# Two splits, three clears and a PSUM bank at the head of the first mixer's projections

## The chip, the cores and the metric

The kernel runs on one core of one Trainium2 chip. The metric is the device time of one execution in microseconds (us); lower is better. Times are compared as medians of several executions, and where the stage is looked at from inside, in one profiled execution.

## The reference, cut to what matters

Two transformer blocks run one after the other on 512 tokens of width 1024, in fp32. The change touches only the head of the first block's mixer:

```python
mod = (silu(c) @ w_ada + b_ada)                    # shift1, scale1, gate1, ...
h = rms_norm(x, norm1_w) * (1.0 + scale1) + shift1
p = h @ w_in                                       # 1024 x 3592
qkv = silu(causal_depthwise_conv(p[..., 0:1536], conv_qkv_w))   # four taps
z = p[..., 1536:2048]
a, b = p[..., 2048:2052], p[..., 2052:2056]        # four heads each
g = -exp(a_log) * softplus(a + dt_bias)            # the "row inputs"
beta = sigmoid(b)
# g is summed up inside chunks of 64 tokens, then the gated delta rule runs
```

Everything behind it (gated delta rule, short convolution, output projection, three feed-forward layers, the second block's attention and RWKV mixer) is not touched.

## The kernel before, in words

Activations lie transposed: channels on the partitions, tokens along the free dimension. Every fp32 product is made of three fp32r products. Operand and weight are each split in a high part and a low rest: `HH` and `HL` for the normed input, `WH` and `WL` for the weight.

**Slabs.** Weights come in slabs of 128 x 1024 (one 128-column tile of output, eight k-tiles), in the fixed order `ORDER`, through a ring of four raw buffers `RAW` (the profile's RAWS). Those that are split are numbered in `CUT`: 0 is `ab` (the columns of a and b, 64 wide, half a slab), then `w_in` in the order `IN_ORDER = [4, 5, 6, 7, 0, 1, 2, 3, 8, ...]` as numbers 1, 2, 3 and on. In the text, split number c is called cut c. For each cut ScalarE copies the slab to `WH[c % 3]` (L1767), for which it waits for the matmuls of cut c-3; GpSimd then makes `WL[c % 3]` by four subtractions of 128 x 256 (L2274; two for `ab`) and counts up `w_lo`; TensorE waits for `w_lo` and issues 24 matmuls of 128 x 512, three for each k-tile (L533). SyncE loads the next slab into a raw buffer when that buffer's split is done.

**The head.** The mixer's modulation columns are made first (L568 are its last matmuls, into banks 0 and 1). VectorE reads them (`ada_mod`) and then goes through the norm: for each k-tile a product to `TMP` (L1166), ScalarE's rounding of it to `HH` (L1829), VectorE's rest to `HL` (L1159, counted by `n_lo`). Cut 0 and cut 1 are interleaved on TensorE, k-tile by k-tile: 24 matmuls each, 48 in all. Each k-tile waits for its `n_lo`.

**Banks.** The results of `ab` and of the `w_in` slabs alternate between PSUM banks 0 and 1 by their place in the list `MAIN`: `ab` is place 0 (bank 0), cut 1 place 1 (bank 1), cut 2 place 2 (bank 0). From place 3 on a product waits until the one two places ahead has been read (`cv_tap` for a convolved slab). Place 2 waits for the two readers of `ab`: `row_d.at("tx")` on VectorE (L1239) and `row_a.at("beta")`, a sigmoid on ScalarE (L1883).

**ScalarE in the loop.** For i = 1, 2, ... it makes `WH` of cut i+2 (`begin`), at i = 1 does its part of the row inputs (sigmoid to `ROW`, absolute value, exponential and logarithm in `RT`, `NEA`; two table loads), then `evict(i - 1)`: it copies a finished bank to `STG` (L1852) and its last tap to `TMP` (L1854). From i = 2 on it then applies silu (L1860) and a square (L1863). The `RT` temporaries lie in `TMP[0]` and `TMP[1]`, so the tap of slabs 0 to 2 waits for `row_d.at("rg")`, VectorE's scan of the row inputs (L1251), the last reader of `RT`. VectorE does the row inputs' own steps (L1239, L1242, L1246, L1251) ahead of its first convolution (L1225, three instructions a slab).

**GpSimd at the head.** It adds up the squares, waits for the last modulation column (`ada_col.at(1)`), clears `STG` edges, `ROW` and `ST` (L2299 to L2301), and then starts to split slabs.

Of the kernel before, what the change touches and what calls it, by code (L numbers as in the profile page):

```python
# [59 lines left out]
IN_ORDER = [4, 5, 6, 7, 0, 1, 2, 3] + list(range(8, 28))  # L60
# [20 lines left out]
CUT = {}  # L81
# [46 lines left out]
def finish(stream):  # L128
    for _ in stream:
        pass  # L130
# [12 lines left out]
def program(nc, xT, metaT, cols, consts, slabs, lup, gup, out):  # L143
    f32, f32r = mybir.dt.float32, mybir.dt.float32r
    ALU, ACT = mybir.AluOpType, mybir.ActivationFunctionType
    ve, ae, ge, te, se = nc.vector, nc.scalar, nc.gpsimd, nc.tensor, nc.sync
# [5 lines left out]
    def steps(name, *names):  # L152
        return Steps(sem(name), *names)

    def count(name):
        return Count(sem(name))

    def sbuf(name, shape, dt=f32, st=top):
        return st.enter_context(nc.sbuf_tensor(name, shape, dt))


    PS = top.enter_context(nc.psum_tensor("PS", [128, 8, 512], f32))
# [4 lines left out]
    def bank(i):  # L167
        return PS[:, i, :]
# [16 lines left out]
    TMP = [sbuf(f"TMP{i}", [128, T2]) for i in range(3)]  # L185
# [18 lines left out]
    Z = sbuf("Z", [128, 4, 512], st=m1)  # L204
    YS = sbuf("YS", [128, 4, 512], st=m1)
    ROW = sbuf("ROW", [64, 512], st=m1)
    NEA = sbuf("NEA", [4, 1], st=m1)
    STG = [sbuf(f"STG{i}", [128, 3 + 512], st=m1) for i in range(2)]
    RT = [TMP[i][0:64, 0:512] for i in range(2)]
    COLT = sbuf("COLT", [128, 4, 64], st=m1)  # L210
    EGC = sbuf("EGC", [128, 4, 4], st=m1)
    BEG = sbuf("BEG", [128, 4, 4], st=m1)
# [97 lines left out]
    ada_acc, ada_col, ada_mod = count("ada_acc"), count("ada_col"), count("ada_mod")  # L310
# [13 lines left out]
    n_h, n_hi, n_lo, n_out = count("n_h"), count("n_hi"), count("n_lo"), count("n_out")  # L324
# [9 lines left out]
    cv_ev, cv_tap, cv_si = count("cv_ev"), count("cv_tap"), count("cv_si")  # L334
    cv = steps("cv", "t0", "t1", "t2")
    row_d = steps("row_d", "tx", "sp", "gg", "rg")
    row_a = steps("row_a", "beta", "abs", "exp", "ln", "nea")
# [43 lines left out]
    rg = [steps(f"rg{i}", "c1", "c2") for i in range(2)]  # L381
# [20 lines left out]
    def col(name, i=0, p0=0, p1=128):  # L402
        return CV[p0:p1, COLS[name] + i:COLS[name] + i + 1]
# [117 lines left out]
    def tensor():  # L521
# [67 lines left out]

        def main_bank(what, j):  # L590
            i = MAIN_AT[what, j]
            if i == 2:
                te.wait_ge(*row_d.at("tx"))
                te.wait_ge(*row_a.at("beta"))
            elif i > 2:
                te.wait_ge(*main_read(*MAIN[i - 2]))
            return bank(i % 2)
# [530 lines left out]
    def vector():  # L1128
# [107 lines left out]
        for i in range(1, 10):  # L1236
            if i == 1:
                ve.wait_ge(*gemm.at(CUT["ab", 0]))
                ve.tensor_scalar(RT[0][0:4, :], PS[0:4, 0, :], col("dtb", 0, 0, 4), None,  # L1239
                                 ALU.add).then_inc(*row_d.up("tx"))  # L1240
                ve.wait_ge(*row_a.at("ln"))
                ve.scalar_tensor_tensor(RT[0][0:4, :], RT[0][0:4, :], 0.0, RT[1][0:4, :], ALU.max,  # L1242
                                        ALU.add).then_inc(*row_d.up("sp"))
                ve.wait_ge(*row_d.at("sp"))
                ve.wait_ge(*row_a.at("nea"))
                ve.tensor_scalar(RT[0][0:4, :], RT[0][0:4, :], NEA[:, 0:1], -1.0, ALU.mult,  # L1246
                                 ALU.mult).then_inc(*row_d.up("gg"))
                ve.wait_ge(*row_d.at("gg"))
                ve.wait_ge(*zeros.at("row"))
                ve.wait_ge(s_k1, 32)  # L1250
                ve.tensor_tensor_scan(ROW[0:4, :], YS[0:4, 0, :], RT[0][0:4, :], 0.0, ALU.mult,  # L1251
                                      ALU.add).then_inc(*row_d.up("rg"))
                ve.wait_ge(*row_d.at("rg"))
            finish(convolve(i - 1))
            if i == 3:
                ve.wait_ge(*row_t.at(0))
                ve.tensor_copy(COLT[:, :, :], h4(PS[:, 2, 0:256])).then_inc(*row_c.up("colt"))
            elif i == 5:
                ve.wait_ge(*row_e.at(0))
                ve.tensor_tensor(BEG[:, :, :], EGC[:, :, :], COLT[:, :, 32:36], ALU.mult).then_inc(*row_c.up("beg"))  # L1260
            elif i == 8:
                finish(unit_heads(0))
# [493 lines left out]
    def scalar():  # L1756
# [13 lines left out]
        def begin(which, j, ahead=2, cap=len(CUTS)):  # L1770
            split_to(min(CUT[which, j] + ahead, cap))
# [72 lines left out]
        def evict(i):  # L1844
            j = IN_ORDER[i]
            b = bank(MAIN_AT["w", j] % 2)
            ae.wait_ge(*gemm.at(CUT["w_in", j]))
            if i >= 2:
                ae.wait_ge(*cv.at("t2", i - 2))
            else:  # L1850
                ae.wait_ge(*zeros.at(f"stg{i}"))
            ae.activation(STG[i % 2][:, 3:515], b, ACT.Copy).then_inc(*cv_ev.up(i))  # L1852
            ae.wait_ge(*(cv_si.at(i - 3) if i >= 3 else row_d.at("rg")))
            ae.activation(TMP[i % 3][:, 0:512], b, ACT.Identity, scale=col("convq", 36 + j)).then_inc(*cv_tap.up(i))  # L1854

        def silu(i):
# [20 lines left out]
        begin("w_in", IN_ORDER[0], 1)  # L1877
        for i in range(1, 10):
            begin("w_in", IN_ORDER[i], 1)
            if i == 1:  # L1880
                ae.wait_ge(*gemm.at(CUT["ab", 0]))
                ae.wait_ge(*zeros.at("row"))
                ae.activation(ROW[32:36, :], PS[32:36, 0, :], ACT.Sigmoid).then_inc(*row_a.up("beta"))  # L1883
                log_and_exp()
                ae.wait_ge(*row_d.at("tx"))
                ae.activation(RT[1][0:4, :], RT[0][0:4, :], ACT.Abs).then_inc(*row_a.up("abs"))
                ae.wait_ge(*row_a.at("abs"))
                ae.activation(RT[1][0:4, :], RT[1][0:4, :], ACT.Exp, scale=-1.0).then_inc(*row_a.up("exp"))
                ae.wait_ge(*row_a.at("exp"))
                ae.activation(RT[1][0:4, :], RT[1][0:4, :], ACT.Ln, bias=1.0).then_inc(*row_a.up("ln"))  # L1890
                ae.activation(NEA[:, :], col("alog", 0, 0, 4), ACT.Exp).then_inc(*row_a.up("nea"))
            evict(i - 1)
            if i == 7:
                begin("w_in", IN_ORDER[8], 1)
                finish(l2_roots(0))
            if i > 1:
                silu(i - 2)
            if i == 4:
                ae.wait_ge(*row_c.at("colt"))
                ae.activation(EGC[:, :, :], COLT[:, :, 0:4], ACT.Exp).then_inc(*row_e.up(0))  # L1900
# [10 lines left out]
        def evictions():  # L1911
            for i in (10, 11):
                yield i - 10
                evict(i)
            for u in range(4):
                yield 2 + u
                ae.wait_ge(*gemm.at(CUT["w_in", 12 + u]))
                ae.activation(Z[:, u, :], bank(MAIN_AT["w", 12 + u] % 2), ACT.Copy).then_inc(*z_ev.up(u))
            for u in range(4):
                yield 6 + u  # L1920
                ae.wait_ge(*gemm.at(CUT["w_in", 16 + 3 * u]))
                ae.wait_ge(*row_d.at("rg"))
                ae.activation(YS[:, u, :], bank(MAIN_AT["w", 16 + 3 * u] % 2), ACT.Copy).then_inc(*sc_ev.up(u))
            for u in range(4):
                yield 10 + u
                ae.wait_ge(*sc.at("y", u))
                ae.wait_ge(*gemm.at(CUT["w_in", 27]))
                ae.activation(HH[:, 4 + u, NM:T2], YS[:, u, :], ACT.Copy).then_inc(*cat1_hi.up(u))
# [334 lines left out]
    def gpsimd():  # L2263
        split = [0]

        def split_to(c):

            while split[0] <= min(c, len(CUTS) - 1):
                s, i = split[0], LOAD[CUTS[split[0]]]
                n = ORDER[i][2]  # L2270
                ge.wait_ge(*w_hi.at(s))
                for a in range(0, n, 256):
                    p = slice(a, a + 256)
                    ins = ge.tensor_tensor(WL[s % NS][:, p], RAW[i % NR][:, p], WH[s % NS][:, p].bitcast(f32),  # L2274
                                           ALU.subtract)
                ins.then_inc(*w_lo.up(s))
                split[0] += 1
# [8 lines left out]
        def add_squares(q, n, *tiles):  # L2286
            for k in tiles:
                ge.wait_ge(*squared(q, k))
                if k > 1:
                    ge.wait_ge(*added(q, k - 1))  # L2290
                ge.tensor_tensor(SQA[:, 0:n], SQA[:, 0:n], TMP[k % 3][:, 0:n],  # L2291
                                 ALU.add).then_inc(*n_acc.up(added(q, k)[1] - 1))


        ge.memset(EPSC[:, :], EPS).then_inc(*epsc.up(0))
        add_squares(0, T1, *range(1, 7))
        ge.wait_ge(*ada_col.at(1))
        for i in range(2):
            ge.memset(STG[i][:, 0:3], 0.0).then_inc(*zeros.up(f"stg{i}"))  # L2299
# [304 lines left out]
```

## Time and profile before

| what | value |
|---|---|
| median of 3 runs | 1966.74 us (1963.08 to 1975.59) |
| the profiled execution's own time | 1970.3 us |
| its span in the trace | 1969.1 us |
| TensorE busy in the span | 1892.1 us (96%) |
| mean granted TensorE clock | 0.984 |

The span is the trace's, from the first to the last instruction, and 1.2 us shorter than the execution's own time. The profiled execution stands 3.6 us above the median and inside the range of the runs. Engines in the rows are PE (TensorE), PEld (its weight loads), DVE (VectorE), ACT (ScalarE), POOL (GpSimd), SP (SyncE).

### The profile page before, as it was taken

The numbers are of one execution on the slowest core, as the hardware profiler recorded it, in microseconds if no ns is written. First come the engines' busy times: TensorE is split into PE (matmuls) and PEld (weight loads), VectorE is DVE, ScalarE is ACT, GpSimd is POOL, SyncE is SP. The second block draws the span as 40 slices with busy tenths as digits, with TensorE's granted clock in tenths as the row PEclk, the third lists the DMA queues.
The fourth block names the chain that finished last, engine by engine and source line by source line (L and its number), as shares of the span: only waits on it lengthen the run. The fifth ranks groups of instructions, "written<-read, shape, count | busy, mean of one in ns | idle before, by whom it ended". The sixth has DMA issues, their size and how long they took to land.

```text
span 1969.1 us, 32734 instructions
## 1 busy us (share of the span) xinstructions
PE 1892.1 (96%) x13848; PEld 1618.7 (82%) x13848; DVE 688.7 (35%) x1066; ACT 688.7 (35%) x1048; POOL 960.6 (49%) x1262
## 2 busy tenths in 40 slices
PE   5999999999999999999999999998999899999998
PEld 4777887677888888999999999997776678888886
DVE  6466564222111011232220025666776432222101
ACT  3653222332322234222222233426665442222222
POOL 3553222645545565655555555543332655555553
PEclk8999998999999999999999999999999999999999
DMA  7243421323332332332232242210001423332321
GB/s 298 75 144 134 140 77 34 107 78 143 123 97 89 93 96 80 103 92 92 86 92 90 89 144 86 81 33 8 3 3 38 146 86 97 93 96 91 97 95 66
DMA packets 54690, 182.75 MB, mean 93 GB/s; under 512 B 6512, under 2 KB 6768, under 8 KB 54416
## 3 DMA queue, kind: packets, MB, share of 16 engines
q1 hardware_dynamic: 54544, 180.65, 28.5%
q8 instruction: 110, 1.80, 0.4%
q14 instruction: 36, 0.29, 0.0%
HBM read 175.39 MB, written 5.24 MB: 92 GB/s over the span
## 4 chain that ended last, share of the span: by engine, by line
PE 88%; DVE 4%; DMA 3%; ACT 2%; issue 2%; POOL 1%; SPq 0%; DVEq 0%; ACTq 0%
PE PS L533 74%; PE PS L655 4%; POOL WL L2274 1%; DMA ADA<-w_ada 1%; PE PS L1054 1%; PE PS L1049 1%; PE PS L1071 1%; DMA RAWS<-w_f0g 1%; DMA xsave<-X 1%; PE PS L797 0%; PE PS L568 0%; PE PS L790 0%; PE PS L794 0%; PE PS L1059 0%; PE PS L782 0%
## 5 line engine op out<-in xcount | busy, mean ns | idle before, releaser
L2274 POOL TENSOR_TENSOR WL<-RAWS,WH 128x256 fp32r<-128x256 f32 x1074 | 827.8, 802 | 738.4 <-ACT WH L1767 738.0
L533 PE MATMUL PS<-HH,WH 128*128 128x264 f32 (+2 forms) x2184 | 665.9, 346 | 31.5 <-POOL WL L2274 13.1
L533 PE MATMUL PS<-HL,WH 128*128 128x264 f32 (+2 forms) x2184 | 655.2, 342 | 0.0
L533 PE MATMUL PS<-HH,WL 128*128 128x264 f32 (+2 forms) x2184 | 653.2, 341 | 0.0
L1767 ACT ACTIVATE WH<-RAWS 128x1024 fp32r<-128x1024 f32 (+2 forms) x275 | 283.9, 1034 | 515.9 <-PE PS L533 436.5
L533 PEld LDWEIGHTS PS<-HH,WH 128*128 128x128 f32 (+1 forms) x2184 | 377.2, 190 | 95.1 <-issue 29.0
L533 PEld LDWEIGHTS PS<-HH,WL 128*128 128x128 f32 (+1 forms) x2184 | 378.1, 190 | 48.6 <-issue 0.6
L533 PEld LDWEIGHTS PS<-HL,WH 128*128 128x128 f32 (+1 forms) x2184 | 378.1, 190 | 48.0 <-issue 1.6
L533 PE MATMUL PS<-IHf,WH 128*128 128x512 f32 (+1 forms) x704 | 209.4, 338 | 0.0
L533 PE MATMUL PS<-IHf,WL 128*128 128x512 f32 (+1 forms) x704 | 209.3, 338 | 0.0
L533 PE MATMUL PS<-ILf,WH 128*128 128x512 f32 (+1 forms) x704 | 209.2, 338 | 0.0
L1487 DVE TENSOR_TENSOR TMP<-TMP,PS 128x512 f32<-128x512 f32 (+1 forms) x66 | 45.8, 693 | 323.2 <-PE PS L533 307.1
L2056 ACT ACTIVATE IHf<-TMP 128x512 fp32r<-128x512 f32 (+1 forms) x66 | 42.0, 636 | 285.2 <-DVE TMP L1487 285.2
L533 PEld LDWEIGHTS PS<-ILf,WH 128*128 128x128 f32 x704 | 120.6, 188 | 14.9
L533 PEld LDWEIGHTS PS<-IHf,WH 128*128 128x128 f32 x704 | 120.5, 188 | 14.9
L533 PEld LDWEIGHTS PS<-IHf,WL 128*128 128x128 f32 x704 | 120.4, 188 | 14.7
L1494 DVE SCALAR_TENSOR_TENSOR X<-PS,X 128x528 f32<-128x528 f32 (+1 forms) x16 | 11.2, 699 | 222.5 <-PE PS L533 222.5
L2291 POOL TENSOR_TENSOR SQA<-SQA,TMP 128x512 f32<-128x512 f32 (+1 forms) x39 | 53.1, 1362 | 65.3 <-ACT TMP L1787 64.5
L1475 DVE TENSOR_TENSOR TMP<-PS,RSTD 128x528 f32<-128x528 f32 (+1 forms) x44 | 30.8, 700 | 151.2 <-PE PS L533 150.5
L1489 DVE TENSOR_TENSOR ILf<-TMP,IHf 128x512 fp32r<-128x512 f32 (+1 forms) x66 | 47.1, 714 | 46.4 <-ACT IHf L2056 46.4
L1482 DVE TENSOR_TENSOR TMP<-TMP,RSTD 128x528 f32<-128x528 f32 (+1 forms) x44 | 36.7, 833 | 41.0 <-ACT TMP L2052 41.0
L1787 ACT ACTIVATE TMP<-X 128x512 f32<-128x512 f32 (+1 forms) x42 | 26.0, 624 | 57.6 <-DVE X L1494 30.7
(487 smaller groups left out, 1718.4 us busy)
## 6 DMA issues: line engine op xcount, KB each, us to landing
RAWS<-w_w_in SPq DMA_DIRECT2D x52, 512.0 KB, 3.6
RAWS<-w_ada SPq DMA_DIRECT2D x32, 512.0 KB, 4.5
RAWS<-w_f0g SPq DMA_DIRECT2D x22, 512.0 KB, 3.6
RAWS<-w_f0u SPq DMA_DIRECT2D x22, 512.0 KB, 3.6
RAWS<-w_f1g SPq DMA_DIRECT2D x22, 512.0 KB, 3.5
RAWS<-w_f1u SPq DMA_DIRECT2D x22, 512.0 KB, 3.5
RAWS<-w_f2g SPq DMA_DIRECT2D x22, 512.0 KB, 3.5
RAWS<-w_f2u SPq DMA_DIRECT2D x22, 512.0 KB, 3.5
```

The lines of the kernel that those rows point to most:

```text
L533: ins = te.matmul(ps[0:m, q, o:o + b - a] if len(halves) > 1 else ps[0:m, o:o + b - a], w[:, k * m:k * m + m], v[:, k0 + k, a:b], start=fi ...
L655: ins = te.matmul(h4(b[:, 0:256])[q, u, :], lhs[q, u, :], con("ident")[q, q] if rhs is None else rhs[q, u, :], start=True, stop=True)
L1049: te.matmul(head_bank(r, c)[:, 0:n], KA[half, i, 128 * j:128 * j + 128], QA[half, i, 512 - n:512], start=True, stop=True).then_inc(*hp[c][ ...
L1475: ve.tensor_tensor(tv, place(f, 2 * j), r, ALU.mult).then_inc(*ff_g.up("g", FT * (f - 1) + j))
L1482: ve.tensor_tensor(tv, tv, r, ALU.mult).then_inc(*ff_g.up("r", FT * (f - 1) + j))
L1487: ve.tensor_tensor(tv, tv, place(f, 2 * j + 1), ALU.mult).then_inc(*ff_mul.up(FT * f + j))
L1489: ve.tensor_tensor(IL[f][:, j, :], t, IH[f][:, j, :].bitcast(f32), ALU.subtract).then_inc(*ff_lo.up(FT * f + j))
L1767: ae.activation(WH[s % NS][:, 0:n], RAW[i % NR][:, 0:n], ACT.Copy).then_inc(*w_hi.up(s))
L1787: ae.activation((TMP[k % 3] if k else SQA)[:, 0:n], X[:, k, t0:T2], ACT.Square).then_inc(*n_sq.up(8 * SQUARED[q] + k))
L2056: ae.activation(IH[f][:, j, :], t, ACT.Copy).then_inc(*ff_hi.up(FT * f + j))
L2274: ins = ge.tensor_tensor(WL[s % NS][:, p], RAW[i % NR][:, p], WH[s % NS][:, p].bitcast(f32), ALU.subtract)
L2291: ge.tensor_tensor(SQA[:, 0:n], SQA[:, 0:n], TMP[k % 3][:, 0:n], ALU.add).then_inc(*n_acc.up(added(q, k)[1] - 1))
```

## The change

GpSimd splits cuts 0 and 1 ahead of its wait for the modulation column and of its clears. `ab` is computed into bank 7. Place 2 of `MAIN` (cut 2, bank 0) then waits only for the first modulation column's reader. The `RT` temporaries move to the buffer `Z`, which is not otherwise in use until the z slabs are evicted; the eviction of the first z slab gets a wait for `row_d.at("rg")` instead, and the taps of slabs 0 to 2 wait for the last `HL` of the norm (`n_lo.at(7)`). On ScalarE, `evict(i - 1)` stands ahead of the row inputs' work and no longer behind it.

```diff
-    RT = [TMP[i][0:64, 0:512] for i in range(2)]
+    RT = [Z[0:64, i, :] for i in range(2)]
...
         def main_bank(what, j):
             i = MAIN_AT[what, j]
+            if what == "ab":
+                return bank(7)
             if i == 2:
-                te.wait_ge(*row_d.at("tx"))
-                te.wait_ge(*row_a.at("beta"))
+                te.wait_ge(*ada_mod.at(0))
             elif i > 2:
                 te.wait_ge(*main_read(*MAIN[i - 2]))
             return bank(i % 2)
...
-                ve.tensor_scalar(RT[0][0:4, :], PS[0:4, 0, :], col("dtb", 0, 0, 4), None,
+                ve.tensor_scalar(RT[0][0:4, :], PS[0:4, 7, :], col("dtb", 0, 0, 4), None,
                                  ALU.add).then_inc(*row_d.up("tx"))
...
             ae.activation(STG[i % 2][:, 3:515], b, ACT.Copy).then_inc(*cv_ev.up(i))
-            ae.wait_ge(*(cv_si.at(i - 3) if i >= 3 else row_d.at("rg")))
+            ae.wait_ge(*(cv_si.at(i - 3) if i >= 3 else n_lo.at(7)))
...
         for i in range(1, 10):
             begin("w_in", IN_ORDER[i], 1)
+            evict(i - 1)
             if i == 1:
                 ae.wait_ge(*gemm.at(CUT["ab", 0]))
                 ae.wait_ge(*zeros.at("row"))
-                ae.activation(ROW[32:36, :], PS[32:36, 0, :], ACT.Sigmoid).then_inc(*row_a.up("beta"))
+                ae.activation(ROW[32:36, :], PS[32:36, 7, :], ACT.Sigmoid).then_inc(*row_a.up("beta"))
                 log_and_exp()
...
                 ae.activation(NEA[:, :], col("alog", 0, 0, 4), ACT.Exp).then_inc(*row_a.up("nea"))
-            evict(i - 1)
...
                 ae.wait_ge(*gemm.at(CUT["w_in", 12 + u]))
+                ae.wait_ge(*row_d.at("rg"))
                 ae.activation(Z[:, u, :], bank(MAIN_AT["w", 12 + u] % 2), ACT.Copy).then_inc(*z_ev.up(u))
...
         add_squares(0, T1, *range(1, 7))
+        split_to(CUT["w_in", IN_ORDER[0]])
         ge.wait_ge(*ada_col.at(1))
         for i in range(2):
             ge.memset(STG[i][:, 0:3], 0.0).then_inc(*zeros.up(f"stg{i}"))
```


## Rows read from the trace of the kernel before

**Rows 1.** The page: busy time by engine; shares of the ending chain

```profile
PE 1892.1 (96%) x13848; PEld 1618.7 (82%) x13848; DVE 688.7 (35%) x1066; ACT 688.7 (35%) x1048; POOL 960.6 (49%) x1262
...
PE 88%; DVE 4%; DMA 3%; ACT 2%; issue 2%; POOL 1%; SPq 0%; DVEq 0%; ACTq 0%
```

**Rows 2.** TensorE's timeline, 33 to 42 us: start, duration, instruction [idle before <-releaser]

```profile
33.57 3.71 PE L568 MATMUL PS<-KC,ACC 128*128 128x1 f32 x32
40.91 0.66 PE L533 MATMUL PS<-HH,WH 128*64 128x512 f32 x1 [3.62 <-DVE HL L1159]
```

**Rows 3.** GpSimd's timeline, 37 to 62 us

```profile
37.41 0.52 POOL L2300 MEMSET ROW<- 64x512 f32 x1
...
38.35 6.39 POOL L2274 TENSOR_TENSOR WL<-RAWS,WH 128x256 fp32r<-128x256 f32 x6
51.71 2.82 POOL L2274 TENSOR_TENSOR WL<-RAWS,WH 128x256 fp32r<-128x256 f32 x4 [6.97 <-ACT WH L1767]
58.77 2.77 POOL L2274 TENSOR_TENSOR WL<-RAWS,WH 128x256 fp32r<-128x256 f32 x4 [4.24 <-ACT WH L1767]
```

**Rows 4.** ScalarE's timeline, 35 to 71 us

```profile
35.07 1.56 ACT L1767 ACTIVATE WH<-RAWS 128x512 fp32r<-128x512 f32 x2
...
49.96 0.72 ACT L1829 ACTIVATE HH<-TMP,MOD 128x512 fp32r<-128x512 f32 x1 [0.60 <-DVE TMP L1166]
...
57.63 1.06 ACT L1767 ACTIVATE WH<-RAWS 128x1024 fp32r<-128x1024 f32 x1 [6.00 <-PE PS L533]
58.71 1.28 ACT L1883 ACT_TABLE_LOAD   x1
...
63.97 0.60 ACT L1852 ACTIVATE STG<-PS 128x512 f32<-128x512 f32 x1
66.36 0.69 ACT L1854 ACTIVATE TMP<-PS,CV 128x512 f32<-128x512 f32 x1 [1.79 <-DVE ROW L1251]
...
70.59 0.63 ACT L1860 ACTIVATE QKV<-TMP 128x512 f32<-128x512 f32 x1
```

**Rows 5.** VectorE's timeline, 37 to 74 us

```profile
37.72 1.91 DVE L1166 SCALAR_TENSOR_TENSOR TMP<-X,SC,RSTD 128x512 f32<-128x512 f32 x2
39.55 1.21 DVE L1159 SCALAR_TENSOR_TENSOR HL<-TMP,MOD,HH 128x512 fp32r<-128x512 f32 x1
...
48.52 0.74 DVE L1159 SCALAR_TENSOR_TENSOR HL<-TMP,MOD,HH 128x512 fp32r<-128x512 f32 x1
...
65.11 1.21 DVE L1251 TENSOR_TENSOR_SCAN ROW<-YS,TMP 4x512 f32<-4x512 f32 x1
67.19 6.15 DVE L1225 SCALAR_TENSOR_TENSOR TMP<-STG,CV,TMP 128x512 f32<-128x512 f32 x6 [0.87 <-ACT TMP L1854]
```

**Rows 6.** TensorE's timeline, 44 to 112 us

```profile
44.80 0.79 PE L533 MATMUL PS<-HH,WH 128*128 128x512 f32 x1 [2.38 <-POOL WL L2274]
...
57.84 0.40 PE L533 MATMUL PS<-HH,WL 128*128 128x512 f32 x1
60.69 0.51 PE L533 MATMUL PS<-HH,WH 128*128 128x512 f32 x1 [2.45 <-issue]
...
67.90 0.40 PE L533 MATMUL PS<-HH,WH 128*128 128x512 f32 x1
...
73.98 0.50 PE L533 MATMUL PS<-HH,WH 128*128 128x512 f32 x1
```

**Rows 7.** The ending chain, 0 to 130 us: start, duration, what

```profile
94.38 5.59 PE PS L533 x24
```

**Rows 8.** Windows: PE, PEld, DVE, ACT, POOL busy; granted clock, DMA

```profile
44.80:50.40 5.60, 5.60 (x13) 3.80 (x14) 5.60 (x9) 2.72 (x5) 0.00 (x0) 0.50 0.27 94
60.70:64.00 3.30, 3.30 (x9) 2.59 (x10) 0.11 (x1) 3.20 (x6) 0.84 (x2) 0.54 0.40 89
...
220.00:400.00 180.00, 174.19 (x1332) 139.75 (x1331) 84.88 (x155) 56.18 (x90) 62.46 (x78) 0.93 0.27 89
```

**Rows 9.** ScalarE's timeline, 100 us

```profile
99.99 0.60 ACT L1852 ACTIVATE STG<-PS 128x512 f32<-128x512 f32 x1 [5.71 <-PE PS L533]
```

## The prediction

> **What bounds the kernel.** I read the page first: TensorE is busy for 96% of the span, and 88% of the ending chain is its work, so only what closes a gap of TensorE, or its clock, can move the time [rows 1]. Then I followed the ending chain, and TensorE's timeline, through the stage of the edits. There are two gaps. The last modulation matmuls end at 33.57 + 3.71 = 37.28, cut 0's first k-tile starts at 40.91, released by HL [rows 2], and behind its three matmuls TensorE idles 2.38 us until 44.80, released by WL [rows 6]: GpSimd began to split at 38.35, behind its clears, and ended the sixth piece at 44.74 [rows 3]. The second gap lies between 57.84 (the start of the last of the 48 matmuls; a pitch later, 58.07) and 60.69, 2.62 us. The trace names no releaser ("issue") [rows 6], but the wait that stands there is the one for the sigmoid, and ScalarE's order gives its time: table load from 58.71, sigmoid behind it, and the next thing at 63.97 [rows 4]. WL of cut 2 had ended at 54.53 [rows 3], so it wasn't that.
>
> Both gaps also cost clock. From 44.80 to 50.4 the granted clock was 0.50, which is 1.2 GHz, and 13 matmuls took 5.60 us; from 60.70 to 64.0 it was 0.54 [rows 8]. A slab at full clock (2.4 GHz) is 24 matmuls in 5.59 us, a pitch of 0.233 [rows 7].
>
> **1. Splits ahead of the clears.** ScalarE has both WH by 35.07 + 1.56 = 36.63 [rows 4], cut 0's about 1.05 us before that. GpSimd, then free, makes cut 0's two pieces from 35.6, at 0.7 us each as in rows without VectorE beside them (2.77 for four [rows 3]): done at 37.1. Cut 1's four begin at once; one is done before VectorE's norm starts at 37.72 [rows 5], the other three run beside it at the pace of before, (6.39 - 0.72) / 5 = 1.13 us [rows 3]: done at 41.2. HL of k-tile 0 came at 39.55 + 1.21 = 40.76 [rows 5]; its first product ran beside the clears at about 0.7 us and now meets a split, which makes it 1.21, the HL row's length, so HL comes at about 41.2 as well. TensorE starts at 41.2, not at 40.91, but doesn't stop after three matmuls. The norm then feeds a k-tile per 2 x 0.67 us (instructions of 0.74 that overlap a little [rows 5]), while TensorE takes 6 x 0.233 = 1.4 at full clock and 2.6 at half: the norm stays ahead.
>
> The price of a collision can be read as a rule too. Rows: a norm instruction of VectorE takes 1.21 beside a split and 0.74 alone [rows 5]. The Trainium skill, page "SBUF — State Buffer", section "SBUF: two separate sides", says that VectorE with two SBUF inputs and a GpSimd instruction that reads SBUF exclude each other for the whole instruction. By that rule the pair would take 0.67 + 0.7 = 1.37 us in turns, HL would come about 0.7 later and the sum below would be 6.5; the trace has a pair in 1.13, and I go by the trace.
>
> How long the clock stays low from 41.2 isn't in the trace. Its two restarts bound it: from 44.80, 45 matmuls took 13.27 us, which is 13.27 - 45 x 0.233 = 2.8 over full clock; from 60.69 a slab took 67.90 - 60.69 = 7.21, which is 1.6 over [rows 6, 7]. So 48 matmuls from 41.2 end at 41.2 + 11.2 + (1.6 to 2.8) = 54.0 to 55.2. No row is clearly nearer (the first has the place, the second the unbroken run), so I take 54.6, and the gain is **3.5 us (2.9 to 4.1)**.
>
> The clears come at about 41 and take 1 us (0.52 for the larger two [rows 3]). They cover themselves: STG and ROW are needed only when the 48 matmuls are through, at 54; ST much later. VectorE loses nothing to them.
>
> **2. ab in bank 7.** Cut 2 needs then only WL and a read of bank 0 that was over before the norm. WL of cut 2 hangs on ScalarE, which makes its WH behind the norm's last HH, at 49.96 + 0.72 [rows 4]. VectorE meets three or four splits in place of six, 0.47 us each, so this comes about 1.3 earlier, 49.4, and with 1.05 for WH and 2.82 for the split [rows 3] WL is there at 53.3. That is 0.7 to 1.9 ahead of need. So the 2.62 us go, and with them the low clock of cut 2, 7.21 - 5.59 = 1.62: **4.2 us**. Cut 3 would start at 54.6 + 5.6 = 60.2, against 67.90.
>
> **3. The eviction ahead of the row inputs.** On ScalarE the block keeps its price, 63.97 - 58.71 = 5.26 us, and is still in front of WH of cut 4. What is late next is here. Cut 0 ends 0.44 before cut 1 (57.63 against 58.07 [rows 4, 6]), so WH of cut 3 runs 54.2 to 55.2, its split to 58.1 (needed at 60.2). Eviction 0 takes about 1.2 and frees bank 1 at 56.5 (needed at 60.2; had it stayed behind the block, it would have come at 61.7 at the earliest). Block until 61.7, WH of cut 4 until 62.8, its split in 2.8 alone or 3.3 beside VectorE: 65.6 to 66.1. Needed when cut 3 and the row transposes are over, 60.2 + 5.6 + 0.5 = 66.3. It fits by 0.2 to 0.7.
>
> Cut 5 doesn't quite. VectorE's scan ended 65.11 + 1.21 = 66.32 [rows 5], 2.35 behind the block; now 64.1. Convolution 0 is half of 6.15 [rows 5]: 67.1. ScalarE's silu and square wait for it and WH of cut 5 stands behind them: from silu's start at 70.59 [rows 4] that is 0.63 + 0.63 + 1.05, so 69.4. The split ends at 72.2 to 72.7. Cut 4 ends at 66.3 + 5.6 = 71.9. A new wait of 0.3 to 0.8: **minus 0.5 us**, too short beside the gaps that cost clock before. For cut 6, WH is behind one eviction and one silu (72.0 + split: under 76) and needed at 78; from there each has more than 1 us in hand.
>
> **4. Waits added.** n_lo(7), the norm's last HL, stands ahead of the taps of slabs 0 to 2 on ScalarE, with WH of the next cut queued behind and VectorE's convolution and bank 1 depending on it; but HL is over before 51.5, the first tap comes at 55.9. The wait for rg stands ahead of the z evictions, which free the banks for cuts 15 and on; the first z slab is cut 13, six slabs of at least 5.59 us behind the one at 94.38 [rows 7], so not before 120, and rg comes at 64. Both cost nothing.
>
> **Sum.** 3.5 + 4.2 - 0.5 = **7.2 us**, with bounds 2.9 + 4.2 - 0.8 = 6.3 and 4.1 + 4.2 = 8.3. I let it through to the end whole: at 99.99 ScalarE has idled 5.71 us for TensorE [rows 9], so the later engines take their time from TensorE there, and raw loads start by freed buffers, not by the clock on the wall. Against the profiled execution, 1970.3 - 7.2 = 1963.1; that one was 3.6 above the median of the runs, so in the measure of the median 1966.7 - 7.2 = **1959.5 us**.
>
> **Rivals.**
> *A. A second low-clock gap (gain about 3).* If cut 4's or cut 5's WL is late by 2.5 us and not 0.5, TensorE makes that gap, its clock falls as it did at 60.69, and the price is 2 more plus 1.6: gain 7.2 - 3.6 = 3.6, time about 1963. For it: the margins of part 3 are 0.2 to 0.7 and hang on ScalarE's order. Against: each term of them is a measured row. The same time comes out if the "issue" gap isn't the sigmoid's wait, so that the change doesn't do what it says: then only part 1 remains.
> *B. Absorbed (no gain, 1967).* Behind 110 us the queues of three engines follow a hand-written order; a wait there that doesn't hang on TensorE would swallow the lead. For it: TensorE is only 174.19 busy of 180 between 220 and 400 [rows 8]. Against: rows 9.
> *C. Slower, by the clock.* In 220 to 400 the mean granted clock is 0.93 though TensorE is hardly idle [rows 8]: short products of the delta rule. That is 0.07 x 180 = 12.6 us. Everything there lands 7 us earlier; if these low stretches fall worse and double, it costs 12.6, net +5.4, about 1972. It decides from a mean of 0.93 - 7.2 / 180 = 0.89 downwards; above it there is still a gain. Against: nothing in that stage changes its own order. By the same token it may give 2 or 3 us.
>
> **Chances.** Forecast (gain 5 to 10) 0.68; A 0.14; B 0.10; C 0.08. The range 1953 to 1969 takes the forecast with its bounds, 3 us either way for the median of a few runs that spread over 12 us, A and most of B. 1% is 19.7 us, about what a measurement of this kernel can tell from no change; nothing in this stage is that large, so within 1% has 0.94 and each side 0.03.
>
> **What would show it.** In the new profile: splits from about 35.6, ahead of the clears; matmuls of L533 without a break from about 41.2 through cut 3, the clock rising once, before 48; cut 2 starting at 54 to 55.2; the sigmoid behind the first STG; a wait of under 1 us ahead of cut 5; the slab that started at 94.38 [rows 7] starting at about 87.2. If it starts at 87 and the end isn't 7 us earlier, B or C is right; if it starts at 90 or later, A. The forecast is wrong if WL of cut 2 or cut 4 is late enough to drop the clock again, or if the clock stays low for much longer than 6 us from 41.2.

## The result, and the profile after

Over 20 runs of each the changed kernel has a median of 1962.72 us against 1967.57. The ratio is 0.9968, with a 95% interval of 0.9957 to 0.998: 6.3 us less (3.9 to 8.5). 7.2 less was forecast. The ratio isn't that of the two medians, which lie 4.9 us apart (0.9975); that, too, is inside the interval. The median itself, 1962.72, stands 3.2 us above the 1959.5 forecast. A second set of runs gave 0.9971 (0.9957 to 0.9985).

The ending chain of the changed kernel, from the modulation matmuls on (start, duration, what), answers to [rows 2, 6, 7]. Line numbers behind the edit are one or two higher than before (L1167 is the former L1166).

```profile
33.91 6.63 PE PS L568 x32
...
40.97 0.76 DVE TMP L1167
...
41.76 0.73 ACT HH L1830
...
42.51 0.76 DVE HL L1160
43.28 0.14 issue
43.41 24.83 PE PS L533 x96
68.24 0.39 PE PS L618 x4
68.63 1.01 issue
69.64 5.79 PE PS L533 x24
75.44 0.84 issue
76.28 11.41 PE PS L533 x48
87.69 3.43 PE PS L609 x8
91.12 5.59 PE PS L533 x24
```

Both old gaps are gone: 96 matmuls, cuts 0 to 3, are one piece, where before 42 and 48 stood apart. Two short gaps are new, 1.01 us ahead of cut 4 and 0.84 ahead of cut 5. The slab that started at 94.38 starts at 91.12, though, 3.3 us earlier and not 7.2. The first line says why: the 32 modulation matmuls, which the change doesn't touch, were twice as slow, 6.83 us on TensorE's timeline (6.63 of them on the chain) against 3.71 [rows 2]. These two executions don't start the stage alike. What the change adds beside them are GpSimd's splits, from 35.90 on:

```profile
35.90 4.16 POOL L2276 TENSOR_TENSOR WL<-RAWS,WH 128x256 fp32r<-128x256 f32 x6 [14.78 <-ACT WH L1768]
```

So I took both kernels once more. The kernel before (its chain from 36 us on, so that its first line is only the end of L568) now had the long modulation matmuls too, 6.83 us on TensorE's timeline, without any split beside them:

```profile
35.91 4.49 PE PS L568 x21
...
41.50 6.36 POOL WL L2274 x6
...
47.91 12.34 PE PS L533 x42
...
63.40 12.86 PE PS L533 x48
...
93.56 3.43 PE PS L608 x8
96.99 3.03 PE PS L533 x13
```

and the changed kernel the short ones, 3.81 us (its chain, also from 36 us on):

```profile
35.95 1.87 PE PS L568 x15
...
38.30 2.30 DVE TMP L1167 x2
40.60 1.15 DVE HL L1160
41.75 0.14 issue
41.88 25.06 PE PS L533 x96
66.94 0.39 PE PS L618 x4
67.33 1.02 issue
68.35 5.82 PE PS L533 x24
74.17 0.82 issue
74.99 11.43 PE PS L533 x48
86.42 3.43 PE PS L609 x8
89.85 5.62 PE PS L533 x24
```

That gives a fair measure: the time from the end of the modulation matmuls (start and duration on TensorE's timeline) to the start of cut 7 (on the chain), compared at equal length of L568. L608 and L609 are one and the same line, the products just ahead of cut 7.

| kernel | L568, us | its end | cut 7 | difference | matmuls at half pace | rest of the span |
|---|---|---|---|---|---|---|
| before | 3.71 | 37.28 | 94.38 | 57.10 | 22 | 1874.7 |
| before, again | 6.83 | 40.40 | 96.99 | 56.59 | 19 | 1867.3 |
| changed | 6.83 | 40.54 | 91.12 | 50.58 | 12 | 1872.0 |
| changed, again | 3.81 | 37.81 | 89.85 | 52.04 | 13 | 1876.0 |
| splits alone | 3.94 | 37.61 | 91.38 | 53.77 | 17 | 1870.3 |
| all but the splits | 6.83 | 40.65 | 95.12 | 54.47 | 13 | 1870.0 |
| eviction behind | 4.05 | 38.03 | 88.32 | 50.29 | 6 | 1871.7 |
| WH of cut 4 ahead | 3.92 | 37.42 | 88.74 | 51.32 | 12 | 1866.8 |
| WH of cuts 4, 5 ahead | 6.83 | 40.61 | 89.10 | 48.49 | 12 | 1868.1 |
| the same, again | 6.83 | 40.95 | 89.54 | 48.59 | 12 | 1871.1 |
| the same, with fillers | 6.83 | 40.82 | 88.47 | 47.65 | 1 | 1872.8 |
| fillers, again | 3.72 | 37.80 | 86.43 | 48.63 | 3 | 1873.4 |

The change is worth 57.10 - 52.04 = 5.1 us with short and 56.59 - 50.58 = 6.0 us with long modulation matmuls. Both lie in the interval of the timed runs. "Half pace" counts L533 rows of 0.60 to 0.69 us on TensorE's timeline. The last column, span less cut 7's start, scatters over 9 us, and by 7 between the two executions of the kernel before: one pair of spans says nothing on a change of this size.

### The profile page after: what moved, and what is told of

Read it like the earlier page. It is cut to its first block, busy times and chain, and to the rows that moved or that the text cites. A ratio compares the mean times of both kernels' runs of the same rounds, so it can differ in the third digit from the quotient of the medians.

```text
span 1963.1 us, 32737 instructions
## 1 busy us (share of the span) xinstructions
PE 1893.5 (96%) x13848; PEld 1622.6 (83%) x13848; DVE 685.2 (35%) x1066; ACT 688.1 (35%) x1048; POOL 961.0 (49%) x1262
## 4 chain that ended last, share of the span: by engine, by line
PE 90%; DVE 3%; ACT 2%; DMA 2%; issue 1%; POOL 1%; SPq 0%; DVEq 0%; ACTq 0%
PE PS L533 75%; PE PS L656 4%; DMA ADA<-w_ada 1%; PE PS L1055 1%; PE PS L1050 1%; PE PS L568 1%; PE PS L1072 1%; POOL WL L2276 1%; DMA RAWS<-w_f0g 1%; DMA xsave<-X 0%; PE PS L783 0%; PE PS L791 0%; PE PS L795 0%; PE PS L798 0%; PE PS L1060 0%
## 5 line engine op out<-in xcount | busy, mean ns | idle before, releaser
L533 PE MATMUL PS<-HH,WH 128*128 128x264 f32 (+2 forms) x2184 | 664.7, 346 | 26.3 <-POOL WL L2276 9.1
L533 PE MATMUL PS<-HL,WH 128*128 128x264 f32 (+2 forms) x2184 | 653.4, 341 | 0.0
L533 PE MATMUL PS<-HH,WL 128*128 128x264 f32 (+2 forms) x2184 | 651.5, 340 | 0.0
L533 PEld LDWEIGHTS PS<-HH,WH 128*128 128x128 f32 (+1 forms) x2184 | 376.7, 190 | 89.2 <-issue 29.9
L533 PEld LDWEIGHTS PS<-HH,WL 128*128 128x128 f32 (+1 forms) x2184 | 377.3, 190 | 48.0 <-issue 0.4
L533 PEld LDWEIGHTS PS<-HL,WH 128*128 128x128 f32 (+1 forms) x2184 | 377.6, 190 | 47.5 <-issue 1.6
L533 PE MATMUL PS<-IHf,WH 128*128 128x512 f32 (+1 forms) x704 | 209.4, 338 | 0.0
L533 PE MATMUL PS<-IHf,WL 128*128 128x512 f32 (+1 forms) x704 | 209.3, 338 | 0.0
L533 PE MATMUL PS<-ILf,WH 128*128 128x512 f32 (+1 forms) x704 | 209.2, 338 | 0.0
L533 PEld LDWEIGHTS PS<-ILf,WH 128*128 128x128 f32 x704 | 120.7, 188 | 14.8
L533 PEld LDWEIGHTS PS<-IHf,WH 128*128 128x128 f32 x704 | 120.5, 188 | 14.9
L533 PEld LDWEIGHTS PS<-IHf,WL 128*128 128x128 f32 x704 | 120.4, 188 | 14.8
```

What stands on the lines that cost most here:

```text
L533: ins = te.matmul(ps[0:m, q, o:o + b - a] if len(halves) > 1 else ps[0:m, o:o + b - a], w[:, k * m:k * m + m], v[:, k0 + k, a:b], start=fi ...
```

## The experiments

**Splits alone.** The kernel before with only this:

```diff
         add_squares(0, T1, *range(1, 7))
+        split_to(CUT["w_in", IN_ORDER[0]])
         ge.wait_ge(*ada_col.at(1))
```

> The kernel before with only the two early splits. Theory (each part's gain as forecast): TensorE runs the 48 matmuls of cuts 0 and 1 without the stop behind the third, so they end 3.5 us earlier (2.9 to 4.1) for equal modulation matmuls; the gap ahead of cut 2 stays at about 2.6 us with the sigmoid behind it. Time 3 to 4 us below the kernel before, ratio about 0.998. Rival (the early splits cost TensorE its clock in the modulation matmuls, as in the changed kernel's profile, where the 32 of L568 took 6.83 us and not 3.71): those matmuls take 6.8 us here too, the norm starts 3.3 us later, and the time is the same as before, ratio 1.000.

L568 took 3.94 us with the splits in front, so they don't set its clock. 57.10 - 53.77 = 3.3 us gained, 3.5 forecast; ratio 0.9973 (0.9959 to 0.9988). This is one profiled execution, as is each row of the table. The old gap ahead of cut 2 stayed:

```profile
41.56 0.66 PE L533 MATMUL PS<-HH,WH 128*64 128x512 f32 x1 [3.96 <-DVE HL L1159]
...
57.85 0.77 PE L533 MATMUL PS<-HH,WH 128*128 128x512 f32 x1 [2.46 <-issue]
```

**All but the splits.** The changed kernel without that line.

> The changed kernel without the two early splits. Theory: the stop behind the third matmul is back, cut 2 follows cut 1 without a gap and at full clock, gain 4.2 us less what cuts 4 and 5 wait, about 2 to 4 us below the kernel before, ratio 0.998 to 0.999. L568 takes 3.7 or 6.8 us by chance, as in any kernel. Rival (early splits set the clock of L568): here L568 takes 3.7 us, since the splits are behind it.

L568 took 6.83 us without early splits: the other half of the answer. 56.59 - 54.47 = 2.1 us; ratio 0.9976 (0.9963 to 0.999). 3.3 and 2.1 make 5.4, between the 5.1 and 6.0 of the whole: the parts add up. In this run the waits ahead of cuts 4 and 5 are there too, 1.01 and 0.82 us on its chain, so bank 7 by itself brings 2.1 + 1.8 = 3.9 us, for 4.2 forecast.

**The eviction behind the row inputs**, all else as changed:

```diff
             begin("w_in", IN_ORDER[i], 1)
-            evict(i - 1)
             if i == 1:
...
                 ae.activation(NEA[:, :], col("alog", 0, 0, 4), ACT.Exp).then_inc(*row_a.up("nea"))
+            evict(i - 1)
```

> The changed kernel with the first eviction behind the row inputs' work, as it was before. Theory: bank 1 is freed 5.3 us later, at about 64 in the changed kernel's own times, against cut 3's need at 62.5, so TensorE waits 1 to 3 us ahead of cut 3, and may lose clock again (up to 1.6 us); WH of cut 4 isn't later than in the changed kernel, so the waits ahead of cuts 4 and 5 shrink by the same 1 to 2 us. Time 0 to 3 us above the changed kernel. Rival (the order doesn't matter, the waits ahead of cut 4 and 5 absorb it): the same as the changed kernel, start of cut 7 within 0.3 us of it for equal L568.

```profile
61.75 0.50 PE L533 MATMUL PS<-HH,WH 128*128 128x512 f32 x1 [1.42 <-ACT TMP L1855]
67.54 0.46 PE L618 MATMUL PS<-KC,ROW 64*128 64x64 f32 x4
84.73 3.59 PE L609 MATMUL PS<-X,KC 128*128 128x512 f32 x8
```

TensorE waits 1.42 us for the bank ahead of cut 3, as the theory said, and behind it no more. 50.29 us to cut 7 are 1.75 less than the changed kernel's 52.04 at short L568, but here only 6 matmuls ran at half pace and not 13, which is 7 x (0.43 - 0.233) = 1.4 us. The waits say the same without that estimate: 1.42 us here, 1.02 + 0.82 = 1.84 in the changed kernel. So the order is worth nothing, within 0.4 us. Neither text had the 1.75; the rival is the one that is nearly right once the clock is taken out. The ratio to before, 0.9964 (0.9948 to 0.998), is the changed kernel's. Moving the eviction moved a wait from cuts 4 and 5 to cut 3 and back.

**WH of cut 4 ahead of the row inputs**, all else as changed:

```diff
             evict(i - 1)
             if i == 1:
+                begin("w_in", IN_ORDER[2], 1)
                 ae.wait_ge(*gemm.at(CUT["ab", 0]))
```

> The changed kernel with ScalarE's copy for WH of cut 4 moved ahead of the row inputs' work. Theory (the waits ahead of cuts 4 and 5, 1.0 and 0.84 us in the changed kernel, stand at the end of ScalarE's order and GpSimd's split beside VectorE's scan): the wait ahead of cut 4 goes whole; the row inputs' chain is 1.05 us later, which makes convolution 0, silu 0 and WH of cut 5 1 us later but WH of cut 4 is no longer between them, so cut 5's wait stays or grows by up to 1. Net gain 0 to 1.5 us against the changed kernel. Rival (VectorE's convolution 0 sets it): no gain, the whole wait moves to cut 5, 1.8 us there.

The wait ahead of cut 4 is gone, the one ahead of cut 5 has grown from 0.82 to 1.37 us, and cut 7 is 52.04 - 51.32 = 0.7 us nearer:

```profile
66.33 0.46 PE L618 MATMUL PS<-KC,ROW 64*128 64x64 f32 x4
73.92 0.47 PE L533 MATMUL PS<-HH,WH 128*128 128x512 f32 x1 [1.37 <-issue]
```

Both are inside the theory's bounds; of the rival's 1.8 us only a part moved to cut 5. The ratio, 0.9968 (0.9952 to 0.9984), can't show a gain of 0.7 us.

**WH of cuts 4 and 5 one place ahead**, in front of the row inputs and of silu 0:

```diff
             evict(i - 1)
+            if i <= 2:
+                begin("w_in", IN_ORDER[i + 1], 1)
             if i == 1:
```

> The changed kernel with ScalarE's copies for WH of cuts 4 and 5 each moved one place ahead (behind evictions 0 and 1, in front of the row inputs and of silu 0). Theory (both new waits come from WH queued on ScalarE behind work that VectorE paces): both waits vanish, TensorE runs from cut 0 to cut 5 without a stop, cut 7 starts 1.5 to 1.9 us earlier than in the changed kernel for equal L568; time 1 to 2 us below the changed kernel, ratio to before 0.996. Rival (the waits move on to cut 6 or the eviction banks): cut 7 starts as in the kernel with WH of cut 4 first, 5.6 us ahead of before.

The chain has no gap from cut 0 to cut 7:

```profile
43.48 24.88 PE PS L533 x96
68.36 0.39 PE PS L618 x4
68.75 16.92 PE PS L533 x72
85.67 3.43 PE PS L609 x8
89.10 5.59 PE PS L533 x24
```

2.1 us less than the changed kernel (50.58 to 48.49, both with long L568), a little more than the two waits. Ratio to before 0.9951 (0.993 to 0.9971), median 1959.26 us. Taken once more:

> The kernel with WH of cuts 4 and 5 ahead once more. Theory: from the end of L568 to the start of cut 7 it is 48.5 us with L568 slow and 50 us with it fast (52.0 in the changed kernel less the two waits of 1.0 and 0.8 us); ratio to before 0.995 to 0.996, 1.5 to 2 us below the changed kernel. Rival (the first ratio was luck): ratio as the changed kernel's, 0.997.

0.9953 (0.9936 to 0.997), 1959.73 us, 48.59 us to cut 7. L568 was long again, so the 50 us for the short case weren't seen. This version is 8.0 us ahead of before at cut 7, and of the versions run it has, with the next one, the lowest medians. At the end of the program its lead over the changed kernel isn't shown, since the intervals overlap (0.993 to 0.997 against 0.9957 to 0.9985).

**Fillers.** The version above, with products that nobody reads in TensorE's pause:

```diff
         ada_column(1, bank(1))
+        for wait in (None, n_h.at(0), n_hi.at(0), n_h.at(1)):
+            if wait:
+                te.wait_ge(*wait)
+            te.matmul(PS[:, 5, 0:256], con("ones"), SQA[:, 0:256], start=True, stop=True)
```

> As the kernel with WH of cuts 4 and 5 ahead, and four products of 256 columns on TensorE, into bank 5 that nobody reads, in the pause between the modulation matmuls and the first projection. Theory (the 48 matmuls start at half clock because TensorE was idle for 4 us before them, which costs 2.2 to 2.5 us): with work in the pause the matmul pitch is 0.233 us sooner, the number of matmuls at 0.43 us falls from about 12 to under 6, and cut 7 starts 1 to 2 us earlier. Rival (the clock follows something else, so that the fillers only cost): as many matmuls at 0.43 us as before, and where L568 is slow the norm's HL waits for the fillers, up to 1 us later.

> The kernel with the four fillers once more, one look, in the hope of the other length of L568 (3.7 to 4 us). Theory (TensorE's idle pause makes the 48 matmuls start at half clock): in that case the fillers keep the clock, and under 6 matmuls run at 0.43 us; from the end of L568 to the start of cut 7 it is 2 us less than the 48.5 us with WH ahead and no fillers. Rival: 12 or more matmuls at 0.43 us.

```profile
43.93 1.06 PE L591 MATMUL PS<-SQA,KC 128*128 128x256 f32 x2
44.43 0.99 PE L533 MATMUL PS<-HH,WH 128*64 128x512 f32 x1
45.22 0.63 PE L533 MATMUL PS<-HL,WH 128*64 128x512 f32 x1
```

In both executions the half pace is over after a few matmuls, 1 and 3 by the table's count and one of 0.99 us ahead of them. In the long cases without fillers (changed, and WH ahead twice) it was 12 each time. In the short ones it was 13 (changed), 12 (WH of cut 4 ahead), 12 (splits alone, ahead of the old gap) and once 6 (eviction behind), so there the count moves by itself. Products in the pause bring the full pace forward.

They don't keep it, though, and the theory's cause is not borne out: in most executions the clock is gone before the pause begins. In the second execution L568 ends at 37.80, and the granted clock (the third number from the end) is already 0.50 then:

```profile
36.50:37.30 0.80, 0.80 (x10) 0.80 (x9) 0.00 (x0) 0.62 (x1) 0.80 (x2) 1.00 0.00 0
37.60:37.80 0.20, 0.20 (x3) 0.20 (x2) 0.00 (x0) 0.00 (x0) 0.20 (x2) 0.50 0.00 0
37.80:44.00 6.20, 5.43 (x13) 3.43 (x13) 6.09 (x9) 2.30 (x4) 4.48 (x8) 0.50 0.83 287
```

By the means of such windows it fell at about 37.5 here, in the kernel before at 37.1 (L568 ends at 37.28), in the changed kernel's second execution at 37.3 (37.81), with the splits alone at 36.8 (37.61) and with WH of cut 4 ahead at 36.7 (37.42): each time while TensorE was still busy with the 128 x 1 matmuls. Only with the eviction behind did it fall after them, at 38.3 (38.03). The fillers ran at half pace themselves. What lowers the clock during L568 wasn't tested.

The gain at cut 7 is smaller than hoped. With long L568 the 96 matmuls take 22.74 us on the chain for 24.88, but they begin 4.17 us behind L568 and not 2.87, because the fillers run late: 2.1 won, 1.3 lost, and 48.49 - 47.65 = 0.8 us remains, where 1 to 2 were expected. The rival's late start came true as well. With short L568 there is no twin without fillers; 46.5 was expected and 48.63 came, 1.6 less than the 50.2 worked out for such a twin (52.04 less 1.84 of waits). Ratio 0.9951 (0.9934 to 0.9969): from the version without fillers the timed runs can't tell it.

**The two kernels again**, which gave the rows of the first section:

> The changed kernel once more, to see whether L568 takes 6.8 us in it always (rival: the change sets its clock) or also 3.7 to 4 us (theory: chance). If it takes 3.7 to 4, the first projection starts at 41.4, cut 7 at 88 to 88.6 and the shift against the kernel before is 5.8 to 6.4 us; ratio to before as measured, 0.996 to 0.998.

> The kernel before once more, one look. Theory: L568 takes 3.7 or 6.8 us by chance, cut 7 starts at 94.4 or 97.7 accordingly; the rest of the span behind cut 7's start scatters by several us around 1871 with the clock's low stretches. Rival (L568's low clock belongs to the changed kernel): 3.7 us.

That L568's length is chance came out as the theory had it: both kernels show both lengths. The numbers of the first text didn't: with short L568 the changed kernel's first projection started at 41.88 and cut 7 at 89.85, not 88 to 88.6, and the shift is 5.1 us, not 5.8 to 6.4. The sum below says where the rest went. For the kernel before, cut 7 at 96.99 is 0.7 earlier than expected.

## Why the prediction was right, point by point

The forecast was worked out for short modulation matmuls, so the changed kernel's second profile is its test.

- *What bounds the kernel, and the unnamed gap being the sigmoid's wait*: right. The sigmoid's row in the kernel before is the one below; it ends at 60.59, and cut 2 starts at 60.69. With both readers of `ab` out of the way cut 2 follows cut 1 at once, and with the early splits alone the 2.46 us stay. That both gaps cost clock holds for the second only, ahead of which the granted clock was 1.00 up to 60.69. Ahead of the first it had been 0.50 since 37.1, so the stop there didn't lower it but only put off its return. The change has that low stretch too, behind its own start at 41.88.

```profile
60.00 0.59 ACT L1883 ACTIVATE ROW<-PS 4x512 f32<-4x512 f32 x1
```

- *Part 1, splits ahead* (3.5 us): 3.3 measured alone. TensorE starts 4.07 us behind L568, 3.92 were forecast. HL met the splits as read: TMP x2 in 2.30 us and HL in 1.15, done 3.94 behind L568 (41.75). By the rule of the Trainium skill that was weighed there (page "SBUF — State Buffer", section "SBUF: two separate sides") the pair takes an estimated 1.37 us in turns and HL comes 0.7 later. HL came when forecast, so the trace's price was the better one. The 0.15 is the step from HL's end to TensorE's start, the "issue" of 0.14 on the chain, which the forecast left out.
- *Clock from the restart* (2.2 us over full clock, at the middle of two bounds): 96 matmuls took 25.06, which is 2.7 over 22.4; off by 0.5, inside the bounds.
- *Part 2, bank 7* (4.2 us; 3.9 by the run without the early splits): the gap and the second low clock are gone, cut 2 is inside one piece of 96. With long L568, WL of cut 2 was there 11.8 us behind the first matmul (52.34 + 2.83 against 43.41); the 48 matmuls took 13.5.
- *Part 3*: **the term that was mis-sized.** Minus 0.5 us for cut 5, "it fits by 0.2 to 0.7" for cut 4; measured 1.02 + 0.82 = 1.84. The step that failed is the price of cut 4's split, 2.8 us alone or 3.3 beside VectorE. It took 4.63 in both profiles of the changed kernel; the second one's timeline of GpSimd and VectorE stands below. Most of the error could have been read before: with VectorE's convolutions beside it, a split took 8.40 / 2 = 4.20 us in the kernel before (first row below), and 4.18 with the eviction behind, where it all but missed the scan, which ended at 62.88 (second row). A split at about 3.3 stands there too (3.28 us from 77.09 on), but the convolution beside it ended at 78.38. With 4.2 the forecast's own times give 62.8 + 4.2 = 67.0 against 66.3, a wait of 0.7 us where 1.02 came. The rest, about 0.45, is new: the split ran beside VectorE's scan, which it never met in the kernel before. One quarter of it took 1.67 us, and the scan 1.68, not 1.21 [rows 5]. The scan's delay went on to convolution 0 (3.33 us for 3.07), silu 0 and WH of cut 5.

```profile
68.07 8.40 POOL L2274 TENSOR_TENSOR WL<-RAWS,WH 128x256 fp32r<-128x256 f32 x8 [6.53 <-ACT WH L1767]
...
62.72 4.18 POOL L2276 TENSOR_TENSOR WL<-RAWS,WH 128x256 fp32r<-128x256 f32 x4 [4.59 <-ACT WH L1768]
```

The changed kernel, second profile:

```profile
63.62 0.74 POOL L2276 TENSOR_TENSOR WL<-RAWS,WH 128x256 fp32r<-128x256 f32 x1 [4.45 <-ACT WH L1768]
63.76 1.68 DVE L1252 TENSOR_TENSOR_SCAN ROW<-YS,Z 4x512 f32<-4x512 f32 x1
64.31 1.67 POOL L2276 TENSOR_TENSOR WL<-RAWS,WH 128x256 fp32r<-128x256 f32 x1
```

- *The eviction's new place*: I argued that it frees bank 1 5.2 us sooner, and that was so (2.1 us behind the start of WH of cut 3 in the changed kernel, 7.5 with the eviction behind), but what is gained at cut 3 is lost at cuts 4 and 5. As a part of its own it is worth nothing.
- *Sum*: 7.2 forecast, 5.1 at cut 7. 1.3 of the 2.1 are the waits, 0.5 the clock, 0.15 the later start; what is left, about 0.2, fits the slab behind the gap, which took 5.82 us for 5.59. The timed 6.3 (3.9 to 8.5) can't tell 5.1 from 7.2.
- *Rivals.* A (a second low-clock gap): not seen, the gaps of 0.8 and 1.0 left the pace whole. The sign given for A, cut 7 starting at 90 or later, did appear in the first profile (91.12); it had no place for long modulation matmuls, and in the second profile it is 89.85 with no low clock behind either gap, so the sign was a poor one. B (absorbed): 5.1 to 6.0 at cut 7 and 6.3 (3.9 to 8.5) at the end leave it little room (up to 2 us), and the version with 8 us at cut 7 has about 9 at the end. C: the mean granted clock in 220 to 400 was 0.96 and 0.93 in the changed kernel's two profiles and 0.93 [rows 8] and 0.98 in those of before. It moves between executions of one kernel, and no effect of the change shows in it.

## What to carry to other kernels

When a wait is taken away, price what moves up against its new neighbours: a split forecast at 2.8 to 3.3 us ran beside VectorE from end to end and took 4.6, of which 4.2 stood in a row of the old trace, and that, not the order of the eviction, set the next gap. A copy that another engine's next product needs belongs in front of work that only a third engine waits for: two such moves gave 2 us more at cut 7 than the change had. For a stage of 50 us in a program of 2000, compare between two marks inside the trace, at equal clock, and leave the verdict on the end to many runs.

## What was not expected of the hardware

- The modulation matmuls (128 x 1, 32 of them) took 3.7 to 4.1 us in six profiles and 6.83 in six others, of kernels with and without each part of the change. The weight loads say that this is TensorE's clock: 0.19 us each in the short cases and 0.33 in the long ones (below, before and changed), as for L533 at a granted clock of 1.00 and 0.50. The 512-column products just ahead (L553, L556) started 0.85 us apart in all twelve, against 0.43 for the same form at L609, so they ran at half pace, and TensorE rose to 2.4 GHz at their end in six executions and not in the others. Both kernels show both. That moved cut 7's start by 1.3 us (changed kernel) and 2.6 (before), and it is part of the runs' spread.

```profile
L568 PEld LDWEIGHTS PS<-KC,ACC x32: 192/192/337, 32.7 to 37.0; 128*128 128x128 f32 x32
...
L568 PEld LDWEIGHTS PS<-KC,ACC x32: 333/333/337, 32.9 to 40.1; 128*128 128x128 f32 x32
```

- The granted clock isn't always in the trace. In the window of the changed kernel below it reads 1.00, while 11 matmuls took 4.50 us, the pitch of 1.2 GHz (0.43 us from one L533 row to the next). It also reads 1.00 over L553 and L556, at half pace, in all profiles. The pitch of the matmuls is the safer reading.

```profile
43.50:48.00 4.50, 4.50 (x11) 3.04 (x12) 4.50 (x8) 2.23 (x4) 0.00 (x0) 1.00 0.80 294
```

- An instruction of VectorE on 4 partitions (the scan) slows GpSimd's on 128 no less than a full one does. A quarter of a split that takes 0.7 us alone took 1.67 beside the scan (1.21 alone) and 1.13 beside a norm instruction on 128 partitions (0.74 alone).
